# Weighing the values of a head pair in one run of matmuls instead of two

## The chip, the cores and the metric

The kernel runs on one core of one Trainium2 chip. The metric is the time of one execution on the device, in microseconds (us), as the median of several runs. The profile is of one execution taken by the hardware profiler. TensorE, the matmul engine, is called PE in the profile's rows, its weight loads PEld; VectorE is DVE, ScalarE is ACT, GpSimd is POOL, and SP issues DMAs.

## The reference

One inference step of a small diffusion backbone with two layers, over 128 prompt tokens and 512 latent tokens. Each layer normalises its input, projects it, and runs grouped-query attention beside a pooling mixer; an output projection and a gated MLP with a short convolution follow. The attention, which is what the change touches, is this:

```python
def one_block(qi):
    s = jnp.einsum('bqkgd,bskd->bkgqs', qi.astype(jnp.float32), kf) * scale
    p = jax.nn.softmax(s, axis=-1)
    return jnp.einsum('bkgqs,bskd->bqkgd', p, vf).astype(q.dtype)
```

There are 8 query heads of dimension 64 on 2 key heads. A latent block of 128 queries attends to 640 keys: 128 cached ones and 512 latent ones. The prompt's one block attends to its own 128 keys only.

## The kernel before

All tokens lie along the free axis, in five tiles of 128 (tile 0 is the prompt, 1 to 4 the latent tokens). Per layer the program runs the input projection, the attention, the output projection and the MLP, one after the other on TensorE.

The attention is cut into **units**, one for each pair of a query tile b and a head h; `UNITS` lists 40 of them for a layer (`NU`). For each latent tile b there are eight latent units and two prompt units (b equal to 0). A latent unit has five key tiles, a prompt unit one. The prompt units stand as units 0, 1, 14, 15, 24, 25, 34 and 35. Below, a **pair** is two units that follow each other, an even one and the odd one behind it (heads h and h+1 of one tile), named by its even unit.

A unit goes through these operations:

1. `scores(i)` on TensorE (L1781): four matmuls for a latent unit, two for a prompt unit, into the buffer `lin[i % 2]`. It waits until the exponential of unit i-2 is done, which frees the buffer.
2. VectorE takes the row maximum (L1274) and negates and scales it (L1280).
3. ScalarE takes the exponential into `prob[i % 3]` (L853), with the row sum read out behind it (ACTIVATION_READ_ACCUMULATOR).
4. VectorE inverts the sum (L1286) and scales the probabilities (L1288).
5. `transpose_prob(i)` on TensorE (L1794): five transposes (one for a prompt unit) into `pair[2]`. There is one such buffer, so the transposes of unit i wait until ScalarE has emptied it of unit i-1.
6. ScalarE copies it to `prob_place[i % 4]` in SBUF (L866; the rows call it prob_t or tree). This is called the **evacuation** below.
7. `weigh_pair` on TensorE (L1823): for each key tile one matmul for each of the pair's two units, 128 by 64 weights (the values) against 128 columns of transposed probabilities. The two units fill the lower and upper half of the partitions of `pair[3]`. When the last key tile is done, each unit counts up the semaphore `s_o`. These matmuls are fp32, and each leaves two records in the trace, here called passes: 12 for three key tiles, 8 for two, 20 for five. A prompt pair has two matmuls and four passes.

Each engine works its own list in order. On TensorE the list is written by hand, as one loop over **steps** i. Step i weighs, then issues the scores of unit i+2, then transposes unit i-1:

```python
for i in range(NU + 4):
    if i >= 4:
        weigh_pair(i - 4 - i % 2, i % 2)
    if i + 2 < NU:
        scores(i + 2)
    if i in (2, 3):
        keep_busy(2, spare)
    if 1 <= i <= NU:
        transpose_prob(i - 1)
```

So an even step weighs key tiles 0 to 2 of a pair, and the odd step behind it key tiles 3 and 4 of the same pair. For a prompt pair there is only key tile 0, so the odd step weighs nothing. ScalarE's list has, in its turn i, the exponential of unit i and then the evacuation of unit i-2; VectorE's has the maximum of unit i and then the scaling of unit i-1. `keep_busy` issues matmuls whose results nobody reads.

Of the kernel before, what the change touches and what calls it, by code (L numbers as in the profile page):

```python
# [61 lines left out]
def build(nc, x_prompt, x_sample, cache_k, cache_v, c, c_ctx, w_mod, b_mod, norm1_g, w_in,  # L62
# [62 lines left out]
    NU = len(UNITS)  # L125
# [3 lines left out]
    for b in range(1, NT):  # L129
        end = b * (NH + 2) - 1  # L130
        GROUPS += [(1 if b == 1 else end - NH // 2, 0, [b - 1]), (end, b, list(range(NH // 2)))]
    NO = len(GROUPS)
    GROUP_END = {end: i for i, (end, _, _) in enumerate(GROUPS)}

    with ExitStack() as ctx:
# [181 lines left out]
        def o_place(G):  # L317

            _, b, pairs = GROUPS[G]
            at = ((G // 2 + (1 if b == 0 else 0)) % 2) * 512  # L320
            src = pair[3][:, at:at + len(pairs) * P].rearrange("p (t c) -> p t c", t=len(pairs))
            return src, (slice(None), slice(pairs[0], pairs[-1] + 1), slice(b * P, (b + 1) * P))
# [1075 lines left out]
        def _(pe):  # L1398
# [184 lines left out]
            def keep_busy(n, dst=pair[2][:, 0:P]):  # L1583


                for _ in range(n):
                    pe.matmul(dst, ident, ident, start=True, stop=True)  # L1587
# [118 lines left out]
            for L in range(DEPTH):  # L1706
# [60 lines left out]
                def scores(i):  # L1767

                    b, h = UNITS[i]
                    un = L * NU + i  # L1770
                    if i < 2:
                        pe.wait_ge(s_plo, L * NPOOL + NPOOL - 1 + i)
                        pe.wait_ge(s_ks, 4 * (L + 1))
                    else:
                        pe.wait_ge(s_exp, un - 1)
                    pe.wait_ge(s_qs, 2 * L * NQ + h + 1)

                    runs = ((0, 0, 2 * P),) if b == 0 else tuple((TP + a, a, e - a) for a, e in HALVES)
                    for kc, oc, n in runs:
                        for r, kk in enumerate((k_hi, k_lo)):  # L1780
                            ins = pe.matmul(lin[i % 2][:, oc:oc + n], q_st[:, h, b * P:(b + 1) * P],  # L1781
                                            kk[:, h // GRP, kc:kc + n], start=r == 0, stop=r == 1)
                    ins.then_inc(s_s, 1)

                def transpose_prob(i):
                    un = L * NU + i
                    pe.wait_ge(s_prob, un + 1)
                    if i > 0:
                        pe.wait_ge(s_pte, un)
                    else:  # L1790
                        pe.wait_ge(s_val, L + 1)
                        pe.wait_ge(s_kout, L + 1)
                    for kt in range(1 if UNITS[i][0] == 0 else NT):
                        ins = pe.transpose(pair[2][:, kt * P:(kt + 1) * P], prob[i % 3][:, kt * P:(kt + 1) * P], ident)  # L1794
                    ins.then_inc(s_pt, 1)

                def weigh_pair(i, part):

                    b, h = UNITS[i]
                    pos = i // (NH + 2)
                    un = L * NU + i
                    g = h // GRP
                    pe.wait_ge(s_pte, un + 2)
                    if b == 0:

                        if pos > 0:
                            pe.wait_ge(s_olo, L * NO + 2 * pos)
                        c = (pos + 1) % 2 * 512  # L1810
                    else:

                        if h == 0 and pos > 0:
                            pe.wait_ge(s_olo, L * NO + 2 * pos - 1)
                        if h == 0 and pos == 0:
                            pe.wait_ge(s_qsd, 2 * (L + 1))
                        c = (pos % 2) * 512 + h // 2 * P
                    nkt = 1 if b == 0 else NT
                    for kt in range(min(nkt, 3)) if part == 0 else range(3, nkt):
                        vv = val[:, 0, g * HD:(g + 1) * HD] if b == 0 else \  # L1820
                            past[:, 1, g * HD:(g + 1) * HD] if kt == 0 else val[:, kt, g * HD:(g + 1) * HD]
                        for side in range(2):
                            ins = pe.matmul(pair[3][side * HALF:(side + 1) * HALF, c:c + P], vv,  # L1823
                                            prob_place[(i + side) % 4][:, kt * P:(kt + 1) * P],
                                            start=kt == 0, stop=kt == nkt - 1)
                            if kt == nkt - 1:
                                ins.then_inc(s_o, 1)
# [5 lines left out]
                keep_busy(2, spare)  # L1833
                scores(1)
                keep_busy(4, spare)
                for i in range(NU + 4):
                    if i >= 4:
                        weigh_pair(i - 4 - i % 2, i % 2)
                    if i + 2 < NU:
                        scores(i + 2)  # L1840
                    if i in (2, 3):
# [3 lines that stand above are left out]
# [87 lines left out]
```

## Time and profile before

| What | us |
|---|---|
| Median of 3 runs (1461.76 to 1462.82) | 1461.98 |
| The profiled execution, its own time | 1460.13 |
| Its span in the profile | 1458.3 |
| TensorE busy in the span | 1426.2 |
| VectorE busy | 909.5 |
| ScalarE busy | 528.8 |
| GpSimd busy | 390.1 |

The profiled execution's own time is 1.8 us above its span, and the median is 1.9 us above that time. The attention of the first layer lies between about 137 and 217 us of the span, that of the second between about 836 and 916 us. In a timeline row, the first number is the start in us from the span's start, the second the duration, then engine, line, operation, and what it writes and reads; in brackets stands how long the engine sat idle before and who released it, where that is known ("issue" means that the profile shows no one). Rows that follow each other on one line are merged into one with a count (x8).

### The profile page before, as it was taken

Reading aid. Unit: us, or ns where it says so; the run is one execution under the profiler, and the core shown is the slowest. Engines: PE = TensorE matmul, PEld = TensorE weight load, DVE = VectorE, ACT = ScalarE, POOL = GpSimd, SP = SyncE. Lnnn points to the kernel's source line nnn. Section 1 sums busy time; section 2 is a strip of 40 time slices with the busy share of each in tenths; the row PEclk is TensorE's granted clock in tenths of the full one; section 3 lists DMA queues with packets and bytes.
Section 4 is the critical chain, followed back from the end, with each engine's and each line's share of the span. In section 5 each row is a group of like instructions: output and inputs, shape, how many; then the busy total and the mean of one; then the engine's idle time right before and its main releaser. Section 6 shows DMA issues by size and latency. Waiting matters only on the chain.

```text
span 1458.3 us, 25364 instructions
## 1 busy us (share of the span) xinstructions
PE 1426.2 (98%) x10067; PEld 1371.9 (94%) x10067; DVE 909.5 (62%) x1438; ACT 528.8 (36%) x791; POOL 390.1 (27%) x265
## 2 busy tenths in 40 slices
PE   7999999999999999999999999999999999999997
PEld 4888779999999999999999977999999999999997
DVE  3637878897876469785775788259844323444333
ACT  3325872442331122332242578234332112332322
POOL 0145001144431024444214600113423101323321
PEclk9999999999999999999999999999999999999999
DMA  9642004244445324334423200133322222222321
GB/s 342 219 173 77 1 2 145 87 131 140 142 138 154 105 89 158 121 118 153 129 57 86 62 1 1 45 102 116 115 72 83 81 68 73 72 72 72 100 60 73
DMA packets 190719, 147.06 MB, mean 101 GB/s; under 512 B 4256, under 2 KB 178984, under 8 KB 188584
## 3 DMA queue, kind: packets, MB, share of 16 engines
q1 hardware_dynamic: 189152, 144.27, 31.4%
q10 hardware_dynamic: 1480, 1.57, 0.3%
q8 instruction: 62, 1.02, 0.3%
q14 instruction: 25, 0.20, 0.0%
HBM read 142.94 MB, written 2.88 MB: 100 GB/s over the span
## 4 chain that ended last, share of the span: by engine, by line
PE 88%; DVE 7%; ACT 2%; issue 1%; DMA 1%; ACTq 0%; DVEq 0%
PE pair L1404 68%; PE pair L1420 7%; PE pair L1781 3%; PE pair L1823 3%; PE pair L1794 2%; DVE mod_acc L1010 1%; PE pair L1587 1%; DVE in_lo L1076 1%; DVE norm_t L1066 1%; DMA rows<-in_final_norm_g_dram 1%; DVE conv L1326 1%; DVE w_lo L987 1%; PE pair L1702 1%; PE pair L1641 1%; DVE small L1274 1%
## 5 line engine op out<-in xcount | busy, mean ns | idle before, releaser
L1404 PE MATMUL pair<-in_hi,w_hi 128*128 128x384 f32 x1728 | 395.5, 310 | 0.2
L1404 PE MATMUL pair<-in_lo,w_hi 128*128 128x384 f32 x1728 | 393.5, 309 | 0.0
L1404 PE MATMUL pair<-in_hi,w_lo 128*128 128x384 f32 x1728 | 393.4, 309 | 0.0
L1326 DVE SCALAR_TENSOR_TENSOR conv<-pair,vec,conv 128x127 f32<-128x127 f32 x352 | 168.8, 541 | 193.2 <-ACT conv L894 192.9
L1404 PEld LDWEIGHTS pair<-in_hi,w_hi 128*128 128x128 f32 x1728 | 263.6, 188 | 5.3 <-issue 2.9
L1404 PEld LDWEIGHTS pair<-in_lo,w_hi 128*128 128x128 f32 x1728 | 263.7, 188 | 0.0
L1404 PEld LDWEIGHTS pair<-in_hi,w_lo 128*128 128x128 f32 x1728 | 263.7, 188 | 0.0
L602 POOL TENSOR_TENSOR silu_a<-silu_a,conv 128x640 f32<-128x640 f32 x44 | 113.0, 2568 | 534.2 <-DVE conv L1326 534.2
L987 DVE TENSOR_TENSOR w_lo<-w_raw,w_hi 128x1024 fp32r<-128x1024 f32 (+1 forms) x148 | 197.3, 1333 | 64.9 <-ACT w_hi L624 64.6
L894 ACT ACTIVATE conv<-pair,vec 128x640 f32<-128x640 f32 x88 | 77.8, 886 | 407.6 <-PE pair L1404 405.4
L624 ACT ACTIVATE w_hi<-w_raw 128x1024 fp32r<-128x1024 f32 (+1 forms) x82 | 96.9, 1182 | 316.4 <-PE pair L1404 286.1
L1010 DVE SCALAR_TENSOR_TENSOR mod_acc<-mod_raw,cond,mod_acc 128x1024 f32<-128x1024 f32 x112 | 180.1, 1652 | 0.0
L1143 DVE SCALAR_TENSOR_TENSOR x<-pair,mod,x 128x128 f32<-128x128 f32 x80 | 40.3, 545 | 169.5 <-PE pair L1404 169.5
L1404 PE MATMUL pair<-act_hi,w_hi 128*128 128x384 f32 x616 | 140.5, 309 | 0.0
L1404 PE MATMUL pair<-act_hi,w_lo 128*128 128x384 f32 x616 | 140.3, 309 | 0.0
L1404 PE MATMUL pair<-act_lo,w_hi 128*128 128x384 f32 x616 | 140.3, 309 | 0.0
L526 POOL TENSOR_TENSOR ssum<-ssum,sq 128x640 f32<-128x640 f32 x24 | 49.0, 2041 | 309.4 <-ACT sq L648 309.4
L1404 PEld LDWEIGHTS pair<-act_lo,w_hi 128*128 128x128 f32 x616 | 94.0, 188 | 0.0
L1404 PEld LDWEIGHTS pair<-act_hi,w_lo 128*128 128x128 f32 x616 | 94.0, 188 | 0.0
L1404 PEld LDWEIGHTS pair<-act_hi,w_hi 128*128 128x128 f32 x616 | 94.0, 188 | 0.0
L606 POOL TENSOR_TENSOR act_lo<-silu_a,act_hi 128x640 f32 x44 | 84.4, 1919 | 7.5 <-POOL act_hi L604 7.5
L639 ACT ACTIVATE w_hi<-w_raw 128x1024 fp32r<-128x1024 f32 x64 | 67.2, 1050 | 0.0
(198 smaller groups left out, 1805.4 us busy)
## 6 DMA issues: line engine op xcount, KB each, us to landing
w_raw<-in_w_up_dram SPq DMA_DIRECT2D x88, 512.0 KB, 3.7
mod_raw<-in_w_mod_dram SPq DMA_DIRECT2D x64, 512.0 KB, 4.2
w_raw<-in_w_down_dram SPq DMA_DIRECT2D x32, 704.0 KB, 4.6
w_raw<-in_w_in_dram SPq DMA_DIRECT2D x20, 512.0 KB, 3.9
w_first<-in_w_mod_dram SPq DMA_DIRECT2D x8, 1024.0 KB, 14.5
w_raw<-in_w_out_dram SPq DMA_DIRECT2D x16, 512.0 KB, 4.2
mod_raw<-in_w_mod_dram SPq DMA_DIRECT2D x4, 1024.0 KB, 6.6
mod_acc<-in_w_mod_dram SPq DMA_DIRECT2D x4, 1024.0 KB, 6.3
```

The costliest lines, as they stand in the source:

```text
L526: pool.tensor_tensor(ssum[:, :], ssum[:, :], sq_slot(m), ALU.add).then_inc(s_ss, 1)
L602: pool.tensor_tensor(silu_a[:, :], silu_a[:, :], conv[:, 1, :], ALU.mult).then_inc(s_act, 1)
L606: pool.tensor_tensor(act_lo[:, j, :], silu_a[:, :], act_hi[:, j, :].bitcast(F32), ALU.subtract).then_inc(s_alo, 1)
L624: act_e.activation(w_hi[:, s, 0:nk, :], w_raw[:, s, 0:nk, :], ACT.Copy).then_inc(s_whi, 1)
L639: act_e.activation(w_hi[:, s, 0:nk, :], w_raw[:, s, 0:nk, :], ACT.Copy).then_inc(s_whi, 1)
L894: act_e.activation(conv[:, s, :], up_result(g, j, s), ACT.Identity, bias=v(L, V_CONVB, s * NF + g * FG + j), scale=v(L, V_TAP[1], s * NF + ...
L987: dve.tensor_tensor(w_lo[:, s, 0:nk, :], w_raw[:, s, 0:nk, :], w_hi[:, s, 0:nk, :].bitcast(F32), ALU.subtract).then_inc(s_wlo, 1)
L1010: dve.scalar_tensor_tensor(out=mod_acc[:, ci, :], in0=mod_raw[:, s, :], scalar=cond[:, ci, ds(k, 1)], in1=mod_acc[:, ci, :], op0=ALU.mult, ...
L1326: ins = dve.scalar_tensor_tensor(out=conv[:, s, d0:d1], in0=up_result(g, j, s)[:, d0 + sh:d1 + sh], scalar=v(L, V_TAP[t], s * NF + g * FG ...
L1404: ins = pe.matmul(dst[:, a:e], w[:, s, k, :], rhs[:, kk, a:e], start=first and r == 0, stop=last and r == 2)
L1420: ins = pe.matmul(dst[:, a:e], w, rhs[:, a:e], start=start, stop=stop)
L1781: ins = pe.matmul(lin[i % 2][:, oc:oc + n], q_st[:, h, b * P:(b + 1) * P], kk[:, h // GRP, kc:kc + n], start=r == 0, stop=r == 1)
```

## The change

`weigh_pair` loses its second argument. It is called in even steps alone and then runs through all five key tiles of both units; odd steps have only scores and transposes. The loop ends one step earlier, since the last pair is finished in its even step. No operation, buffer or semaphore is added or taken away, and the waits at the head of `weigh_pair` are the same, but are issued once a pair.

```diff
-                def weigh_pair(i, part):
+                def weigh_pair(i):
...
-                    for kt in range(min(nkt, 3)) if part == 0 else range(3, nkt):
+                    for kt in range(nkt):
...
-                for i in range(NU + 4):
-                    if i >= 4:
-                        weigh_pair(i - 4 - i % 2, i % 2)
+                for i in range(NU + 3):
+                    if i >= 4 and i % 2 == 0:
+                        weigh_pair(i - 4)
```

The lists of VectorE, ScalarE and SP are the same as before. On TensorE it looks as follows. First the rows on TensorE in the middle of the first query tile of layer 0, before (prob_t are evacuated probabilities, past and val the cached and new values, sq a probability buffer, cst the identity; 64x128 rows are weighing, each matmul of which gives two records in the trace):

```order
L1794 MATMUL pair<-cst,sq 128x128 x5
L1823 MATMUL pair<-prob_t,past 64x128 x2
L1823 MATMUL pair<-prob_t,val 64x128 x4
L1781 MATMUL pair<-k_hi,q_st 128x384
L1781 MATMUL pair<-k_lo,q_st 128x384
L1781 MATMUL pair<-k_hi,q_st 128x256
L1781 MATMUL pair<-k_lo,q_st 128x256
L1794 MATMUL pair<-cst,sq 128x128 x5
L1823 MATMUL pair<-prob_t,val 64x128 x4
L1781 MATMUL pair<-k_hi,q_st 128x384
L1781 MATMUL pair<-k_lo,q_st 128x384
```

and the same place in the changed kernel:

```order
L1794 MATMUL pair<-cst,sq 128x128 x5
L1822 MATMUL pair<-prob_t,past 64x128 x2
L1822 MATMUL pair<-prob_t,val 64x128 x8
L1781 MATMUL pair<-k_hi,q_st 128x384
L1781 MATMUL pair<-k_lo,q_st 128x384
L1781 MATMUL pair<-k_hi,q_st 128x256
L1781 MATMUL pair<-k_lo,q_st 128x256
L1794 MATMUL pair<-cst,sq 128x128 x5
L1781 MATMUL pair<-k_hi,q_st 128x384
L1781 MATMUL pair<-k_lo,q_st 128x384
```

The four matmuls of key tiles 3 and 4 moved from the odd step to the even one, so that between two runs of transposes there are now only four scores matmuls.

The second place is TensorE in layer 0 where the scores of the prompt units 14 and 15 (two matmuls each) fall into the two steps:

```order
 L1794 MATMUL pair<-cst,sq 128x128 x5
-L1823 MATMUL pair<-prob_t,past 64x128 x2
-L1823 MATMUL pair<-prob_t,val 64x128 x4
+L1822 MATMUL pair<-prob_t,past 64x128 x2
+L1822 MATMUL pair<-prob_t,val 64x128 x8
 L1781 MATMUL pair<-k_hi,q_st 128x256
 L1781 MATMUL pair<-k_lo,q_st 128x256
 L1794 MATMUL pair<-cst,v_feat 128x128 x5
-L1823 MATMUL pair<-prob_t,val 64x128 x4
 L1781 MATMUL pair<-k_hi,q_st 128x256
 L1781 MATMUL pair<-k_lo,q_st 128x256
 L1794 MATMUL pair<-cst,sq 128x128 x5
```

Here only two scores matmuls are left between the transposes.

## Rows read from the trace of the kernel before

**Rows 1.** The page, the chain that ended last: shares of the span by line.

```profile
PE pair L1404 68%; PE pair L1420 7%; PE pair L1781 3%; PE pair L1823 3%; PE pair L1794 2%; DVE mod_acc L1010 1%; PE pair L1587 1%; DVE in_lo L1076 1%; DVE norm_t L1066 1%; DMA rows<-in_final_norm_g_dram 1%; DVE conv L1326 1%; DVE w_lo L987 1%; PE pair L1702 1%; PE pair L1641 1%; DVE small L1274 1%
```

**Rows 2.** Windows (length; busy time of each engine; granted clock), layer 0's attention.

```profile
152.00:216.00 64.00, 61.73 (x568) 49.91 (x568) 50.57 (x140) 51.18 (x109) 0.00 (x0) 1.00 0.01 2
```

**Rows 3.** Timeline, TensorE's weight loads, one even and one odd step of layer 0.

```profile
155.41 0.20 PEld L1823 LDWEIGHTS pair<-prob_t,past 128*64 128x64 f32 x4 [0.17 <-issue]
...
156.21 0.19 PEld L1781 LDWEIGHTS pair<-k_hi,q_st 128*128 128x128 f32 x1 [0.17 <-issue]
...
156.81 0.57 PEld L1794 LDWEIGHTS pair<-cst,sq 128*128 128x128 f32 x5
...
157.54 0.42 PEld L1823 LDWEIGHTS pair<-prob_t,val 128*64 128x64 f32 x8 [0.17 <-issue]
...
158.13 0.19 PEld L1781 LDWEIGHTS pair<-k_hi,q_st 128*128 128x128 f32 x1 [0.17 <-issue]
...
159.46 0.20 PEld L1823 LDWEIGHTS pair<-tree,past 128*64 128x64 f32 x4 [0.17 <-issue]
```

**Rows 4.** Timeline, VectorE and ScalarE at the same place.

```profile
153.44 0.82 DVE L1274 TENSOR_REDUCE small<-pair 128x1 f32<-128x640 f32 x1
...
154.48 0.89 ACT L853 ACTIVATE v_feat<-pair,small,rq 128x640 f32<-128x640 f32 x1
...
155.02 0.82 DVE L1274 TENSOR_REDUCE small<-pair 128x1 f32<-128x640 f32 x1
...
155.27 0.19 ACT L853 ACTIVATION_READ_ACCUMULATOR v_feat<-pair,small,rq 128x1 f32 x1
...
157.10 0.82 DVE L1274 TENSOR_REDUCE small<-pair 128x1 f32<-128x640 f32 x1 [0.41 <-PE pair L1781]
```

**Rows 5.** Timeline, layer 1, an odd step behind a prompt pair, where nothing is weighed.

```profile
873.93 0.58 PEld L1794 LDWEIGHTS pair<-cst,v_feat 128*128 128x128 f32 x5
...
874.78 0.71 ACT L866 ACTIVATE prob_t<-pair 128x640 f32<-128x640 f32 x1
...
874.89 0.19 PEld L1781 LDWEIGHTS pair<-k_hi,q_st 128*128 128x128 f32 x1 [0.39 <-issue]
...
875.60 0.53 PEld L1794 LDWEIGHTS pair<-cst,sq 128*128 128x128 f32 x5
```

**Rows 6.** Timeline, layer 0, four cycles around the prompt pair 14.

```profile
163.52 0.20 PEld L1823 LDWEIGHTS pair<-prob_t,past 128*64 128x64 f32 x4 [0.17 <-issue]
...
164.32 0.19 PEld L1781 LDWEIGHTS pair<-k_hi,q_st 128*128 128x128 f32 x1 [0.17 <-issue]
...
164.57 0.58 PEld L1794 LDWEIGHTS pair<-cst,v_feat 128*128 128x128 f32 x5
...
166.94 0.20 PEld L1823 LDWEIGHTS pair<-tree,past 128*64 128x64 f32 x4 [0.17 <-issue]
...
170.24 0.14 PEld L1794 LDWEIGHTS pair<-cst,v_feat 128*128 128x128 f32 x1
...
170.54 0.20 PEld L1823 LDWEIGHTS pair<-prob_t,past 128*64 128x64 f32 x4 [0.16 <-issue]
...
170.65 0.28 ACT L866 ACTIVATE tree<-pair 128x128 f32<-128x128 f32 x1
...
174.17 0.20 PEld L1823 LDWEIGHTS pair<-tree,val 128*64 128x64 f32 x4 [0.17 <-issue]
...
177.51 0.20 PEld L1823 LDWEIGHTS pair<-prob_t,past 128*64 128x64 f32 x4 [0.17 <-issue]
```

**Rows 7.** Timeline, end of layer 0's attention: weighing of pairs 36 and 38.

```profile
213.51 0.20 PEld L1823 LDWEIGHTS pair<-prob_t,past 128*64 128x64 f32 x4 [0.17 <-issue]
...
216.00 0.20 PEld L1823 LDWEIGHTS pair<-tree,past 128*64 128x64 f32 x4 [0.45 <-ACT tree L866]
```

**Rows 8.** Windows, the start of layer 1's attention.

```profile
842.00:844.00 2.00, 1.12 (x9) 0.88 (x8) 1.90 (x6) 1.54 (x4) 0.00 (x0) 0.97 0.00 0
844.00:846.00 2.00, 2.00 (x11) 2.00 (x10) 1.90 (x5) 1.29 (x5) 0.00 (x0) 0.50 0.00 0
```

## The prediction

> **What bounds the kernel now.** I read the page's chain of waits first, to see whose time the end depends on. Most of it is the large projections (L1404), which the change does not touch. The attention's three lines on TensorE, L1781, L1823 and L1794, are each in the chain with 2 or 3% of the span [rows 1]; what happens to them moves the end. The windows come second: of 64 us of attention TensorE is busy for 61.7, VectorE for 50.6 and ScalarE for 51.2 [rows 2]. So TensorE sets the pace, but the other two are busy four fifths of the time, and a unit goes through all three. The question is thus not only how much work TensorE has, but whether the rhythm of its list suits theirs. That has to be read from the timeline, step by step.
>
> **One cycle (an even and an odd step) as it is** [rows 3], by starts of weight loads. Even step: weighing with 12 passes to the scores, 155.41 to 156.21, 0.80 us; scores 0.60; transposes 0.73 up to the next weighing, of which 0.57 is loading. Odd step: weighing with 8 passes, 157.54 to 158.13, 0.59; then again 0.60 and 0.73. Together 4.05 us, and nobody waits for a semaphore for long: 155.41 to 159.46. From 12 passes in 0.80 and 8 in 0.59 a pass takes 0.0525 us, and what remains at the end of a run is 0.17. The same 0.17 stands as idle time ahead of each weighing and ahead of each scores that follow one [rows 3], but not between scores and transposes. A weighing thus costs its passes and two gaps of 0.17.
>
> **What the change removes.** The odd step's weighing goes, with two gaps: 0.34 us a pair. The 8 passes (0.42 us) only move to the even step. That holds for 15 latent pairs a layer; pair 38 is weighed in one piece now already, since nothing stands between its two parts. If nothing else mattered, 30 pairs by 0.34 would give 10.2 us.
>
> The Trainium skill says in "TensorEngine Tiling (Array Packing)", section Key Properties, that a change of tiling mode (weighing has 64 columns, scores and transposes 128) drains the engine. The 0.17 us agree with that, and by that rule alone the change is a pure gain.
>
> **What it adds: a wait in every odd step.** The transposes of each unit go through one buffer, so between the transposes of unit i-1 and those of unit i lies an evacuation by ScalarE. The kernel before shows this step without weighing already, behind its prompt pairs. There the loads of one unit's transposes end at 873.93 + 0.58 = 874.51, the evacuation runs from 874.78 to 875.49, and the next transposes load at 875.60: 1.09 us after 874.51, of which the scores between them take only 0.60 [rows 5]. The copy itself is 0.71, the hand-over to it 0.27, and back 0.11. There are four such steps between full-size transposes, behind pairs 14 and 24 of each layer; the rows show one, and the other three read the same 1.09. Before, an ordinary odd step puts 0.76 (passes and both gaps) and 0.60 between its transposes, 1.36 in all, so the evacuation is hidden; an even one even more. After, the odd step has 0.60 there and needs 1.09. Of the scores' 0.60 nothing more is won: in-order TensorE stands still for the other 0.49 us. That is the step on which I forecast: the 8 passes were the cover of the evacuation, and they move to a step that had cover already.
>
> **The sum, by kinds of cycle** (weighing start to weighing start).
>
> A: all four operations full size. After: 20 passes and a gap 1.22, scores 0.60, transposes 0.57, evacuation 1.09, transposes 0.57, gap 0.17: 4.22 against 4.05. +0.17, for pairs 4, 6, 16, 26: +0.7.
>
> B: the scores are those of prompt units, 164.57 - 164.32 = 0.25 [rows 6]. After: 1.22 + 0.25 + 0.57 + 1.09 + 0.57 + 0.17 = 3.87; before 163.52 to 166.94, 3.42. +0.45, for 3 pairs (8, 18, 28): +1.35. The wait is longest here, since the shorter scores cover less.
>
> C: the odd step transposes a prompt unit, a single load of 0.14 [rows 6]. After: 1.22 + 0.60 + 0.57 + 1.09 + 0.14 + 0.17 = 3.79; before 3.60 (166.94 to 170.54). +0.19, for 3 pairs: +0.55.
>
> D and E, pairs 12 and 14 and their likes, together 6.97 before (170.54 to 177.51). In D the even step transposes a prompt unit, whose evacuation takes 0.28 instead of 0.70 [rows 6], so the merge saves time there. But then steps follow each other so fast that the softmax chain ends last. From the start of scores to the maximum 0.89 (156.21 to 157.10), from there to the exponential 1.04 (153.44 to 154.48), to the end of its sum 0.98 (to 155.46), back to TensorE 0.11: 3.02 us until the scores two units later may start; two full maxima start 1.58 apart at the closest (153.44 to 155.02) [rows 3, 4]. With the scores of unit 18 at 1.22 after the weighing, those of unit 20 start 3.02 later and those of 21 4.60 later; TensorE's own list would have reached them at 2.5 and about 4.2. Counted from the scores of unit 18, unit 17's transposes end at 3.02 + 0.60 + 0.57 = 4.19, unit 18's wait for the evacuation until 4.19 + 1.09 = 5.28 and end at 5.85, and the next cycle's weighing starts at 1.22 + 5.85 + 0.17 = 7.24. +0.27, with bounds 0 (all chain latencies a little shorter) and +0.6; for three such pairs of cycles +0.8.
>
> End: pair 36, where no scores are left: 1.22 + 0.57 for the last transposes, then the evacuation until pair 38 can be weighed, 0.27 + 0.70 + 0.06: 2.82 against 2.49 [rows 7]. +0.3. Pair 2, at the start, is about 0: there TensorE waits for ScalarE now, and the longer weighing fits into part of that wait.
>
> A layer: 0.7 + 1.35 + 0.55 + 0.8 + 0.3 = 3.7; two layers 7.4. Where the small latencies all come out a few hundredths shorter, A and B lose 0.05 each and D with E 0.1: I take 7.0. The output projection starts right behind the last weighing, and VectorE and ScalarE then wait for its first result, so nothing behind it takes up the delay. The profiled execution would go from 1460.13 to 1467.1 us; the median stands 1.85 above it, 1461.98 + 7.0 = 1469.0.
>
> **Rivals.**
>
> *The gaps win.* If the evacuation were not in the way, the full 0.34 a pair would be back: 1461.98 - 10.2 = 1451.8 us. For it stands that the gaps are real [rows 3]; against it that the step without weighing is in the trace, and waits [rows 5]. It would need an evacuation that starts with the first transpose, and no row shows that. Chance 0.06.
>
> *A draw.* TensorE's own gain and the wait cancel, because the wait is shorter in most odd steps than behind the prompt pairs: with 0.17 less a cycle (0.92 for 1.09), A is 0 and the sum 7.0 - 34 x 0.17 = 1.2 us, thus about 1463. Chance 0.10.
>
> *The clock falls too.* TensorE now stands still a tenth of the time, in C to E more. At the start of layer 1's attention it was busy for 1.12 us of 2, and in the next 2 us the granted clock was 0.50, the lower level of 1.2 GHz; in layer 0's attention it is 1.00 throughout [rows 8, 2]. There half of 2 us of work is lost, 1.0 us. If a fall came with each of the four query tiles of both layers, that is 8 us more: 1477 us. Against it: TensorE will still be busy some 85% of the time. Layer 0's start, where TensorE has little work too, kept its clock. The Trainium skill ("TensorE: Matmul & The Clock Gate", section on a second failure mode) tells of kernels whose frequent short idle times between groups of matmuls made the clock swing; no stretch of this trace with idle times as short as 0.5 us does. Chance 0.10.
>
> **The numbers.** The forecast, 1466 to 1473, has 0.74; the gaps 0.06, the draw 0.10, the clock 0.10. The range takes in half of the draw and the cheaper half of the clock case: 1463.5 to 1475. About 0.2%, 2.9 us, is what a measurement of this kernel can tell from no change; above that, slower, lie the forecast and the clock, 0.84; faster is 0.06, the same 0.10.
>
> **What would show it.** In the profile after: a cycle of kind A of 4.2 us; in every odd step idle time of about 0.5 us ahead of L1794's loads, released by ScalarE's L866, where there is none now; weighing runs of 20 records and 1.22 us; the scores behind transposes start without a gap of 0.17. From the weighing of pair 2 to that of pair 38 some 68.5 us instead of 64.95 in layer 0. The forecast is wrong if odd steps show no such wait, or if the transposes load under 1.0 us behind the previous ones.

## The result, and the profile after

The changed kernel takes 1470.03 us (median of 4 runs, 1467.96 to 1470.53) against 1461.87 us for the kernel before: a ratio of 1.0051, with a 95% interval of 1.0038 to 1.0064. Run a second time on another chip it took 1470.15 us against 1461.88, ratio 1.0049 (1.0036 to 1.0063). The profiled execution took 1467.96 us with a span of 1466.2 us.

The chain that ended last, by line, in the page of the changed kernel; it answers to [rows 1]:

```profile
PE pair L1404 67%; PE pair L1420 7%; PE pair L1822 3%; PE pair L1794 2%; PE pair L1781 2%; DVE mod_acc L1010 1%; PE pair L1587 1%; DVE in_lo L1076 1%; DVE norm_t L1066 1%; ACT prob_t L866 1%; DVE conv L1326 1%; ACT tree L866 1%; DVE small L1274 1%; PE pair L1702 1%; PE pair L1634 1%
```

New in it are ScalarE's evacuations (prob_t and tree, L866). The same shows in the windows of the two attentions (columns as in [rows 2]): TensorE is busy for 60.7 of 69 us, where it was 61.7 of 64, at a full granted clock.

```profile
150.00:219.00 69.00, 60.70 (x588) 51.34 (x587) 51.50 (x145) 52.27 (x111) 0.00 (x0) 1.00 0.01 2
854.00:923.00 69.00, 60.70 (x591) 51.34 (x591) 51.15 (x145) 52.23 (x110) 0.00 (x0) 1.00 0.01 2
```

One full-size cycle in layer 0's timeline, which answers to [rows 3]. Weighing is L1822 now:

```profile
159.15 0.20 PEld L1822 LDWEIGHTS pair<-tree,past 128*64 128x64 f32 x4 [0.17 <-issue]
...
160.39 0.19 PEld L1781 LDWEIGHTS pair<-k_hi,q_st 128*128 128x128 f32 x1 [0.17 <-issue]
...
160.99 0.57 PEld L1794 LDWEIGHTS pair<-cst,sq 128*128 128x128 f32 x5
...
161.52 0.19 PEld L1781 LDWEIGHTS pair<-k_hi,q_st 128*128 128x128 f32 x1
...
161.83 0.70 ACT L866 ACTIVATE prob_t<-pair 128x640 f32<-128x640 f32 x1 [1.00 <-PE pair L1794]
...
162.65 0.53 PEld L1794 LDWEIGHTS pair<-cst,sq 128*128 128x128 f32 x5 [0.48 <-issue]
...
163.35 0.20 PEld L1822 LDWEIGHTS pair<-prob_t,past 128*64 128x64 f32 x4 [0.17 <-issue]
```

The weighing takes 1.24 us; the scores at 161.52 follow the transposes without a gap; and the transposes of the odd step load at 162.65, after 0.48 us of idle time, 1.09 us behind the end of those before (160.99 + 0.57 = 161.56). The loads' row says "issue", but the evacuation ends at 161.83 + 0.70 = 162.53 and they start 0.12 later, the hand-over of [rows 5]. The cycle is 4.20 us, where it was 4.05.

From the weighing of pair 2 to that of pair 38 it is 68.23 us in layer 0 and 68.24 in layer 1 (64.95 and 64.65 before): 6.9 us. Layer 0's pair 2 comes 0.34 earlier. From pair 38 of layer 0 to the first scores of layer 1 it is 621.4 us, where it was 619.8: 1.6 us more, outside the attention. From there to layer 1's pair 2 it is 0.3 less. That makes up the 7.9 us between the two spans; the section on the prediction comes back to the 1.6.

### The profile page after: what moved, and what is told of

It is laid out like the page before. It is cut to its first block, busy times and chain, and to the rows that moved or that the text cites. A ratio compares the mean times of both kernels' runs of the same rounds, so it can differ in the third digit from the quotient of the medians.

```text
span 1466.2 us, 25350 instructions
## 1 busy us (share of the span) xinstructions
PE 1420.0 (97%) x10067; PEld 1371.7 (94%) x10067; DVE 906.9 (62%) x1438; ACT 529.2 (36%) x791; POOL 389.0 (27%) x265
## 3 DMA queue, kind: packets, MB, share of 16 engines
q10 hardware_dynamic: 1480, 1.57, 0.3%
## 4 chain that ended last, share of the span: by engine, by line
PE 86%; DVE 7%; ACT 3%; issue 2%; DMA 1%; SPq 0%; DVEq 0%; ACTq 0%
PE pair L1404 67%; PE pair L1420 7%; PE pair L1822 3%; PE pair L1794 2%; PE pair L1781 2%; DVE mod_acc L1010 1%; PE pair L1587 1%; DVE in_lo L1076 1%; DVE norm_t L1066 1%; ACT prob_t L866 1%; DVE conv L1326 1%; ACT tree L866 1%; DVE small L1274 1%; PE pair L1702 1%; PE pair L1634 1%
## 5 line engine op out<-in xcount | busy, mean ns | idle before, releaser
L602 POOL TENSOR_TENSOR silu_a<-silu_a,conv 128x640 f32<-128x640 f32 x44 | 111.7, 2540 | 536.7 <-DVE conv L1326 536.7
L1010 DVE SCALAR_TENSOR_TENSOR mod_acc<-mod_raw,cond,mod_acc 128x1024 f32<-128x1024 f32 x112 | 179.3, 1646 | 0.7 <-DMA mod_raw<-in_w_mod_dram 0.7
L1274 DVE TENSOR_REDUCE small<-pair 128x1 f32<-128x640 f32 (+1 forms) x80 | 57.0, 713 | 20.8 <-PE pair L1781 20.5
```

Source lines behind the costliest of these rows:

```text
L602: pool.tensor_tensor(silu_a[:, :], silu_a[:, :], conv[:, 1, :], ALU.mult).then_inc(s_act, 1)
L1010: dve.scalar_tensor_tensor(out=mod_acc[:, ci, :], in0=mod_raw[:, s, :], scalar=cond[:, ci, ds(k, 1)], in1=mod_acc[:, ci, :], op0=ALU.mult, ...
L1274: dve.tensor_reduce(small[:, i % 3, 3:4], lin[i % 2][:, 0:nkeys], AX_X, ALU.max).then_inc(s_max, 1)
```

## The experiments

The gap theory says that what counts is the number of changes between 64 and 128 columns of weights. The cover theory says that an evacuation, 1.09 us from transposes to transposes, has to fit under what stands between them. In the tables a cycle is the time from one pair's weighing to the next one's in layer 0's timeline, by kinds as in the prediction; A is the cycle behind pair 4 or 6, E the one behind pair 14. Each ratio is to runs of the kernel before beside it (medians 1461.3 to 1461.9 us), so small differences are better read from the ratios and the cycles than from medians of different chips.

| Kernel | median us | ratio (95%) | A | B | C | D | E |
|---|---|---|---|---|---|---|---|
| before | 1461.87 | 1 | 4.05 | 3.42 | 3.60 | 3.63 | 3.34 |
| changed | 1470.03 | 1.0051 (1.0038 to 1.0064) | 4.20 | 3.85 | 3.75 | 3.33 | 3.86 |
| 4 and 1 key tiles | 1462.84 | 1.0013 (1.0003 to 1.0023) | 4.06 | 3.63 | 3.61 | 3.63 | 3.46 |
| changed, shorter copy | 1466.08 | 1.0031 (1.0018 to 1.0044) | 4.09 | 3.75 | 3.65 | 3.32 | 3.80 |
| before, shorter copy | 1460.01 | 0.9989 (0.9979 to 0.9998) | 4.06 | 3.36 | 3.63 | 3.62 | 3.24 |
| changed, four idle matmuls | 1475.83 | 1.0102 (1.0085 to 1.0118) | 4.60 | 3.84 | 3.76 | 3.33 | 4.70 |
| changed, two idle matmuls | 1471.26 | 1.0060 (1.0046 to 1.0074) | 4.20 | 3.84 | 3.76 | 3.33 | 4.25 |
| changed, scores together | 1472.11 | 1.0068 (1.0051 to 1.0084) | 4.12 | 4.03 | 3.22 | 4.14 | 3.75 |
| changed, shorter maximum | 1467.47 | 1.0044 (1.0027 to 1.0060) | 4.20 | 3.85 | 3.76 | 3.34 | 3.73 |

### Four key tiles and one

```diff
-                    for kt in range(min(nkt, 3)) if part == 0 else range(3, nkt):
+                    for kt in range(min(nkt, 4)) if part == 0 else range(4, nkt):
```

> The kernel before, but with four key tiles in the even step and one in the odd. Number of runs and of gaps as before. Theory (the odd step's transposes wait for the evacuation, 1.09 us from transposes to transposes): the odd step still has 4 passes, two gaps and the scores between transposes, 0.21 + 0.34 + 0.60 = 1.15 us, just over 1.09, so a full-size cycle stays at 4.05 to 4.07 us; where the scores are a prompt unit's 0.25 the cover is 0.80 and the cycle grows from 3.42 to about 3.65. In all +1.5 us, 1463.4. Rival (the long even step itself costs, in proportion to what moves into it): half of the measured loss of the full merge, +4 us, with a full-size cycle of 4.12.

The loads on TensorE in this kernel, weighing of both steps and the odd step's transposes:

```profile
160.36 0.20 PEld L1823 LDWEIGHTS pair<-tree,past 128*64 128x64 f32 x4 [0.17 <-issue]
...
161.97 0.57 PEld L1794 LDWEIGHTS pair<-cst,sq 128*128 128x128 f32 x5
162.71 0.20 PEld L1823 LDWEIGHTS pair<-tree,val 128*64 128x64 f32 x4 [0.17 <-issue]
...
163.68 0.58 PEld L1794 LDWEIGHTS pair<-cst,sq 128*128 128x128 f32 x5
164.42 0.20 PEld L1823 LDWEIGHTS pair<-prob_t,past 128*64 128x64 f32 x4 [0.17 <-issue]
```

From the end of transposes at 162.54 to the next at 163.68 there are 1.14 us, just over the 1.09 of the evacuation, and the cycle has not grown: 4.06. Where the scores are short it grew from 3.42 to 3.63, as expected. The time, +1.2 us, agrees with the cover theory's +1.5. The long even step itself costs nothing.

### A shorter evacuation, in both kernels

```diff
+                        nkeys = min(nkeys, 4 * P)
                         act_e.activation(prob_place[j % 4][:, 0:nkeys], pair[2][:, 0:nkeys], ACT.Copy).then_inc(s_pte, 1)
...
-                                            prob_place[(i + side) % 4][:, kt * P:(kt + 1) * P],
+                                            prob_place[(i + side) % 4][:, min(kt, 3) * P:(min(kt, 3) + 1) * P],
```

> The changed kernel, evacuating only four of five key tiles of a latent unit (the fifth tile of probabilities is left out and the fourth is read in its place; TensorE's work is the same). The copy gets about 0.10 us shorter. Theory: every wait in odd steps gets 0.10 shorter: full-size cycle 4.10, the one with prompt scores 3.76, in all -3.2 to -3.6 us against the changed kernel, about 1466.5. Rival (the loss is in the passes or in the order, not in the copy): no change, 1470.

> The same shorter copy in the kernel before (the fifth tile of probabilities left out). Theory: there the copy is hidden in all cycles but those with prompt scores and those behind prompt pairs: full-size cycle 4.05 as before, in all -1 to -1.8 us, about 1460.5. If the copy were as much in the way as in the changed kernel, -3.5 us, 1458.4.

In the changed kernel with the shorter copy (lines are one further on), an odd step:

```profile
158.17 0.60 ACT L867 ACTIVATE tree<-pair 128x512 f32<-128x512 f32 x1 [0.90 <-PE pair L1795]
...
158.88 0.53 PEld L1795 LDWEIGHTS pair<-cst,v_feat 128*128 128x128 f32 x5 [0.36 <-issue]
```

The copy is 0.60 instead of 0.70, and TensorE's idle time ahead of the transposes 0.36 instead of 0.48. Every kind of cycle with a wait fell by 0.10 to 0.11 (E by 0.06, for a reason that the softmax chain below gives). From pair 2 to pair 38 that is 3.0 us in both layers together; the medians, taken on two chips, differ by 4.0 us. TensorE's work is the same. In the kernel before, the full-size cycle does not answer to the copy at all (4.06), only B and E (and the cycles at the two ends) do, and the time falls by 1.7 us: there the copy is covered. In B it was not quite: the trace of before has 1.09 us from transposes to transposes there too (loads end at 165.15, the next begin at 166.24). This is the plainest of the tests: the same 0.10 us on ScalarE is worth 0.11 in a full-size cycle of one kernel and nothing in the other.

### Idle matmuls in front of the waiting transposes

```diff
+                    if i % 2 and 7 <= i < NU and UNITS[i - 1][0] and UNITS[i - 2][0] and UNITS[i - 3][0] and UNITS[i - 3][1] > 0:
+                        at = ((i - 3) // (NH + 2) % 2) * 512 + UNITS[i - 3][1] // 2 * P
+                        keep_busy(4, pair[3][:, at:at + P])
                     if 1 <= i <= NU:
                         transpose_prob(i - 1)
```

> The changed kernel with four idle matmuls (0.43 us together) ahead of the transposes in 16 odd steps whose two neighbouring transposes are both full size and whose next pair is not the first of its query tile. Theory: TensorE stands still there for 0.48 us anyway, so the time does not change by more than 0.5 us (1470) and the cycles stay 4.20. Rival (TensorE's own work is what has become longer, not a wait): 16 x 0.43 = +7 us, 1477.

Measured were 1475.8 us. The theory's number was off by 6 us; the rival's was close, but by a wrong size of the idle matmuls. The loads of one filled odd step:

```profile
159.11 0.98 PEld L1587 LDWEIGHTS pair<-cst 128*128 128x128 f32 x8
160.00 0.58 PEld L1794 LDWEIGHTS pair<-cst,v_feat 128*128 128x128 f32 x5
```

Four idle matmuls are eight passes and take 0.89 us (159.11 to 160.00), not 0.43. They are fp32 with 128 columns of weights; I had sized them by a stretch in which their records are merged with others. At that size the rival would have been 16 x 0.89 = 14 us; the cycles of the two layers grew by 7.8 together. The full-size cycle grew by 0.40, which is 0.89 less 0.49: the wait paid for the rest. Behind pair 34 no scores are left and the transposes wait the whole 1.09; there the four idle matmuls cost nothing, and the cycle is 3.86 as without them:

```profile
218.82 0.97 PEld L1587 LDWEIGHTS pair<-cst 128*128 128x128 f32 x8
219.95 0.53 PEld L1794 LDWEIGHTS pair<-cst,v_feat 128*128 128x128 f32 x5 [0.15 <-issue]
```

To test that reading and not only to fit it, the same with two:

> As the kernel with four idle matmuls ahead of the transposes in 16 odd steps, but with two. The profile of that kernel shows that an idle matmul is two passes of 0.11 us, so the four were 0.89 us and not 0.43, and a full-size cycle grew by 0.40, which is 0.89 less a wait of 0.49. Two are 0.44 us, just under the wait. Theory: nothing changes, full-size cycle 4.20 to 4.22, total within 0.5 us of the changed kernel beside it. Rival (added work costs a fixed share, 0.45 of its length): +0.20 a cycle, +3.2 us.

```profile
159.01 0.53 PEld L1587 LDWEIGHTS pair<-cst 128*128 128x128 f32 x4
159.56 0.53 PEld L1794 LDWEIGHTS pair<-cst,v_feat 128*128 128x128 f32 x5
160.25 0.20 PEld L1822 LDWEIGHTS pair<-tree,past 128*64 128x64 f32 x4 [0.17 <-issue]
```

Now the transposes follow the idle matmuls almost at once, and the full-size cycle is 4.20 as without them: 0.44 us of work were free. Not free were they behind pair 14 (4.25 for 3.86, the same behind pair 24) and behind pair 2 (4.65 for 4.23), 6 of the 16 places; there most of the wait is elsewhere, ahead of the scores, and has been served when TensorE comes to the transposes (0.39 to 0.42 of the 0.44 is paid). The cycles of the two layers add up to +2.4 us; the median is +1.1 us against the changed kernel beside it on that chip (1470.15), where I had expected under 0.5. The total does not decide against the rival's +3.2, but the cycles do: the added work costs next to nothing or nearly all by its place, not a fixed share.

### The softmax chain

In the changed kernel's timeline, layer 0, the two steps behind the weighing of prompt pair 14 (kind E):

```profile
174.28 0.20 PEld L1822 LDWEIGHTS pair<-tree,val 128*64 128x64 f32 x4 [0.17 <-issue]
175.16 0.19 PEld L1781 LDWEIGHTS pair<-k_hi,q_st 128*128 128x128 f32 x1 [0.69 <-ACT sq L853]
...
175.82 0.53 PEld L1794 LDWEIGHTS pair<-cst,v_feat 128*128 128x128 f32 x5
176.75 0.19 PEld L1781 LDWEIGHTS pair<-k_hi,q_st 128*128 128x128 f32 x1 [0.40 <-ACT sq L853]
...
177.45 0.53 PEld L1794 LDWEIGHTS pair<-cst,sq 128*128 128x128 f32 x5
...
178.14 0.20 PEld L1822 LDWEIGHTS pair<-prob_t,past 128*64 128x64 f32 x4 [0.17 <-issue]
```

Both scores wait for an exponential (sq, L853), the first for 0.69 us. The transposes at 177.45 come 1.10 us behind the end of those before (176.35), about what the evacuation asks, and the scores ahead of them end at about 176.75 + 0.60 = 177.35. So the evacuation ends last there by about 0.1 us only, and both limits act in E; that is why a copy shorter by 0.10 gave only 0.06. The two cycles D and E take 7.19 us, where they took 6.97 [rows 6]. To see whether the chain is what waits there, VectorE's maximum is taken over four of five key tiles:

```diff
-                        dve.tensor_reduce(small[:, i % 3, 3:4], lin[i % 2][:, 0:nkeys], AX_X, ALU.max).then_inc(s_max, 1)
+                        dve.tensor_reduce(small[:, i % 3, 3:4], lin[i % 2][:, 0:min(nkeys, 4 * P)], AX_X, ALU.max).then_inc(s_max, 1)
```

> The changed kernel with the row maximum taken over four of five key tiles (the fifth is left out), 0.13 us shorter on VectorE. Theory: full-size cycles stay 4.20, since the evacuation ends last there; the cycles behind pairs 14, 24 and 34, where the softmax chain ends last, fall from 3.86 to about 3.73; in all -1 us, 1469. Rival (VectorE's load sets the pace everywhere): two maxima a cycle, -0.26 each, -8 us.

The weighing of pair 14 and of pair 16 in that kernel:

```profile
174.37 0.20 PEld L1822 LDWEIGHTS pair<-tree,val 128*64 128x64 f32 x4 [0.17 <-issue]
...
178.10 0.20 PEld L1822 LDWEIGHTS pair<-prob_t,past 128*64 128x64 f32 x4 [0.17 <-issue]
```

3.73 for 3.86, and A, B, C and D as before: the maximum counts in E (and in the first two cycles, by 0.2) and nowhere else. The median is 2.6 us lower, on another chip; against the kernels before beside them the difference is 2.0 us, still more than the 1.2 us that the cycles of both layers add up to, and no larger than the scatter told of below.

The second test of the chain gives every evacuation its cover by the order of the list:

```diff
-                for i in range(NU + 3):
-                    if i >= 4 and i % 2 == 0:
+                for i in range(0, NU + 3, 2):
+                    if i >= 4:
                         weigh_pair(i - 4)
...
+                    if 1 <= i <= NU:
+                        transpose_prob(i - 1)
                     if i + 2 < NU:
                         scores(i + 2)
+                    if i + 3 < NU:
+                        scores(i + 3)
...
-                    if 1 <= i <= NU:
-                        transpose_prob(i - 1)
+                    if i + 1 <= NU:
+                        transpose_prob(i)
```

> The changed kernel with the same work in another order: weighing, transposes, both scores, transposes. Each evacuation is now covered (1.39 us of weighing with its gaps, or 1.20 us of two scores), and TensorE's own list is 3.74 us for a full-size cycle. Theory: not the evacuation but the softmax chain now ends last: the second scores may start only 1.58 + 3.02 = 4.6 us after the first scores of the cycle ahead, which makes full-size cycles of 4.1 to 4.3 us and a total of 1470 to 1473. Rival (only the evacuation stood in the way of the gaps' 0.34 us): cycles of 3.75, total about 1453.

```profile
160.73 0.82 DVE L1274 TENSOR_REDUCE small<-pair 128x1 f32<-128x640 f32 x1 [0.86 <-PE pair L1781]
...
161.76 0.20 PEld L1822 LDWEIGHTS pair<-tree,past 128*64 128x64 f32 x4 [0.17 <-issue]
161.78 0.89 ACT L853 ACTIVATE sq<-pair,small,rq 128x640 f32<-128x640 f32 x1 [0.93 <-DVE small L1280]
...
162.66 0.69 ACT L866 ACTIVATE prob_t<-pair 128x640 f32<-128x640 f32 x1
...
163.47 0.53 PEld L1794 LDWEIGHTS pair<-cst,sq 128*128 128x128 f32 x5 [0.64 <-issue]
```

1472.1 us, full-size cycles of 4.12 to 4.20: not a gain, as the chain theory had it. The rows show one link that I had not named. The transposes wait again (0.64), for an evacuation at 162.66 that stands on ScalarE's list behind an exponential, which waited 0.93 for the maximum of scores issued 1.9 us before. Cover alone does not help when the copy is queued behind the chain. So two things can hold this loop, the evacuation and the softmax chain with ScalarE's list behind it. The full-size cycles of the kernel before waited for neither, and at 4.05 they were as short as this order's.

### The price of a gap

To see that the 0.17 us belong to the change of columns, one idle matmul (128 columns) is set once between the weighing of the two units of a pair and once behind both. Both kernels weigh all key tiles of one unit first, then of the other, in all pairs; 24 pairs have the idle matmul. The diff is of the first; the second has it behind the loop over the two units instead.

```diff
-                    for kt in range(nkt):
-                        vv = ...
-                        for side in range(2):
-                            ins = pe.matmul(...)
+                    for side in range(2):
+                        if side == 1 and b and h < NH - 2 and True:
+                            keep_busy(1, pair[3][:, c + P:c + 2 * P])
+                        for kt in range(nkt):
+                            vv = ...
+                            ins = pe.matmul(...)
```

> The changed kernel, weighing first all key tiles of one unit, then of the other, with one idle matmul of 128 columns of weights between the two for 24 of the pairs. To be read against the next kernel. Theory of the gaps: the idle matmul costs its own 0.11 us and two more gaps of 0.17, 0.45 us a pair in the even step: full-size cycle 4.65, total +10.8 us, 1480.8. Rival (a gap belongs to the semaphore waits ahead of a run, not to the change of the number of columns): +0.11 a pair, cycle 4.31, +2.6 us.

> As the kernel before this one, but with the idle matmul behind the whole weighing, beside the scores, which have the same 128 columns of weights. Both theories: +0.11 us a pair in the even step, full-size cycle 4.31, total +2.6 us, 1472.6. The difference to the kernel before this one is the price of two gaps.

Measured: 1514.4 us (ratio 1.0363, 1.0343 to 1.0383) inside, 1497.9 us (1.0246, 1.0229 to 1.0263) beside. The sizes missed by far, the sign between them held. Inside:

```profile
173.41 0.19 PEld L1824 LDWEIGHTS pair<-tree,past 128*64 128x64 f32 x2 [0.17 <-issue]
173.57 0.90 PEld L1824 LDWEIGHTS pair<-tree,val 128*64 128x64 f32 x8
174.64 0.30 PEld L1587 LDWEIGHTS pair<-cst 128*128 128x128 f32 x2 [0.17 <-issue]
175.06 0.19 PEld L1824 LDWEIGHTS pair<-tree,past 128*64 128x64 f32 x2
175.22 0.90 PEld L1824 LDWEIGHTS pair<-tree,val 128*64 128x64 f32 x8
176.30 0.19 PEld L1781 LDWEIGHTS pair<-k_hi,q_st 128*128 128x128 f32 x1 [0.17 <-issue]
```

and beside:

```profile
172.21 0.19 PEld L1824 LDWEIGHTS pair<-tree,past 128*64 128x64 f32 x2 [0.17 <-issue]
172.38 0.68 PEld L1824 LDWEIGHTS pair<-tree,val 128*64 128x64 f32 x6
172.93 0.19 PEld L1824 LDWEIGHTS pair<-tree,past 128*64 128x64 f32 x2
173.03 0.96 PEld L1824 LDWEIGHTS pair<-tree,val 128*64 128x64 f32 x10
174.16 0.30 PEld L1587 LDWEIGHTS pair<-cst 128*128 128x128 f32 x2 [0.17 <-issue]
174.38 0.19 PEld L1781 LDWEIGHTS pair<-k_hi,q_st 128*128 128x128 f32 x1
```

The idle matmul inside has no semaphore to wait for, and the gap of 0.17 stands before it all the same; behind it, before weighing goes on, another 0.2 (from 174.86, its two passes later, to 175.06). Beside, there is one gap ahead of it and none between it and the scores. So the gap belongs to the change of columns.

Why are both kernels 28 us and more slower? One unit's 10 passes alone take 1.06 us here, 0.106 each, where alternating passes of the two units take 0.0525. Beside, the 20 passes with one gap behind take 1.95 us against 1.24. The plain reading is that the order of the change, key tile by key tile and side by side, lets the two halves of the columns work together. That is not tested apart from a rival: in the other order, matmuls that follow each other also add into the same columns of `pair[3]`. I had not known that this order was worth 0.71 us a pair. Of the difference of 16.5 us between the two kernels, 0.69 us for each of 24 pairs, 0.37 are the two gaps, and the rest is that beside, the second unit's passes can still start beside the first one's last (1.78 us for 20 passes instead of 2.12). The test gave the cause of the gaps, not a clean price; the price is best read as 0.17 from the rows.

### The changed kernel once more

> The changed kernel once more, on the chip of the kernel beside it: 4.20 us for a full-size cycle, total 1468 to 1470.5, ratio to the kernel before 1.005. The runs of the changed kernel so far lie between 1468.0 and 1470.5, those of before within 1.2 us; if the spread sits behind layer 0's attention, where DMAs land just in time, the span between the two attentions differs by 1 to 2 us from one profile to the next and the attentions by less than 0.3.

Median and ratio came as expected. The cycles are the same to 0.04 us but for the last two of layer 1, 4.13 and 4.10 instead of 3.86 and 2.80: together 1.57 us, more than the 0.3 that I had allowed. The windows there:

```profile
918.00:920.00 2.00, 0.86 (x6) 0.68 (x7) 1.50 (x6) 1.88 (x5) 0.00 (x0) 1.00 0.00 0
920.00:922.00 2.00, 2.00 (x17) 1.67 (x18) 0.23 (x1) 0.70 (x1) 0.00 (x0) 0.55 0.00 0
922.00:924.00 2.00, 2.00 (x17) 1.55 (x13) 0.00 (x0) 0.00 (x0) 0.00 (x0) 0.60 0.00 0
```

At the end of the attention, where no scores are left, TensorE was busy for 0.86 of 2 us; then the granted clock was 0.55 and 0.60 over 4 us, the lower of the two levels (1.2 GHz) for most of it. In the first profile of the same kernel it stayed at 1.00 there. The second profile has another fall at the start of layer 1's attention (0.63 and 0.52 from 848 to 852 us), where the kernel before has its own [rows 8].

## Why the prediction was right

The forecast was 1469.0, slower by 7.0; measured were 1470.0, slower by 8.2, and 8.3 in the second comparison.

- **The wait in the odd step** is there as forecast: 1.09 us from transposes to transposes, an idle time of 0.48 (0.49 forecast), no gap between transposes and scores. The shorter copy and the idle matmuls show that it is the evacuation that is waited for.
- **The sum by kinds:** A 4.20 (forecast 4.22), B 3.85 (3.87), C 3.75 (3.79), D with E 7.19 (7.24), the end 2.80 (2.82). Pair 2 fell from 4.36 to 4.23 in layer 0 and rose from 4.09 to 4.24 in layer 1, where I had said about 0 for both. From pair 2 to 38 it is +3.3 us in layer 0 and +3.6 in layer 1, 6.9 in all; 7.4 was summed and 7.0 taken. That 7.0 is a choice and not a sum: taken off every cycle, the allowances that I named make 1.3 us.
- **Nothing behind takes up the delay:** true. But something behind added to it in the profile, and I had not looked for it. From pair 38 of layer 0 to the first scores of layer 1 the twelve profiles here have 619.8 us (four of them, the kernel before among them) or 621.1 to 621.4 (eight, both of the changed kernel among them). (The 0.3 by which the changed kernel's two stand above the other six is mostly a wait of TensorE for ScalarE, 0.3 at L1556.) What parts the eight from the four is one wait of TensorE, the engine that sets the pace, some 93 us behind pair 38, in the MLP. The changed kernel, first profile:

```profile
305.30 3.79 DVE L1010 SCALAR_TENSOR_TENSOR mod_acc<-mod_raw,cond,mod_acc 128x1024 f32<-128x1024 f32 x2
305.46 2.54 POOL L602 TENSOR_TENSOR silu_a<-silu_a,conv 128x640 f32<-128x640 f32 x1 [21.78 <-DVE conv L1326]
...
310.84 1.65 DVE L987 TENSOR_TENSOR w_lo<-w_raw,w_hi 128x1024 fp32r<-128x1024 f32 x1
...
312.54 0.56 PE L1404 MATMUL pair<-in_hi,w_hi 128*128 128x384 f32 x2 [1.42 <-DVE w_lo L987]
```

  and the kernel before at the same place:

```profile
302.09 2.47 DVE L1010 SCALAR_TENSOR_TENSOR mod_acc<-mod_raw,cond,mod_acc 128x1024 f32<-128x1024 f32 x2
302.26 3.74 POOL L602 TENSOR_TENSOR silu_a<-silu_a,conv 128x640 f32<-128x640 f32 x1 [21.76 <-DVE conv L1326]
...
306.31 1.65 DVE L987 TENSOR_TENSOR w_lo<-w_raw,w_hi 128x1024 fp32r<-128x1024 f32 x1
```

  VectorE's two operations L1010 and GpSimd's L602 run at the same time, and one side or the other takes 1.2 to 1.3 us longer, never both. Where it is VectorE, the w_lo behind it is late and TensorE waits for it. In the 24 places (twelve profiles, two layers) the wait of 1.42 to 1.45 us is there in the 11 with the long L1010 and in none of the other 13. It is not bound to the change: the kernel before with the shorter copy has it in layer 0, the changed one with four idle matmuls has it nowhere. The profile of the kernel before has none, the changed kernel's first one (layer 0) and its second two. What tips it is not shown. This wait, worth about 1.3 us each time, and falls of the clock as above are the two sources of scatter that the profiles show; which of them makes the 1.2 between my 7.0 and the 8.2 of the medians stays open, since the runs without a profile do not tell.
- **The rivals.** *The gaps win:* they were saved in fact, but the odd step's wait took 0.49 us where 0.34 were saved and 0.42 of passes moved to the even step, which leaves +0.15 a cycle. Given cover by another order, the loop ran into the softmax chain and the copy queued behind it instead. *A draw:* excluded by the interval; the waits are the same in all odd steps of a kind. *The clock:* not in the middle of the attention, which ran at 1.00 in both profiles of the changed kernel, but at its thin ends. A single fall cost 1.57 us in one profile, more than the 1.0 that I had put down. The Trainium skill (page "TensorE: Matmul & The Clock Gate", section "A second HAM failure mode") tells of a kernel whose frequent short idle times between groups of matmuls made the clock swing. Idle times of 0.48 us in every full-size cycle did not do that here; the fall came after a stretch with idle times of 1.09 and 1.34 us, and the first profile has the same idle times there without a fall.
- **The gaps.** The rule of the Trainium skill that a change of tiling mode drains TensorE ("TensorEngine Tiling (Array Packing)", Key Properties) agrees with the traces, the test with the idle matmul included, with 0.17 to 0.20 us a change. It was right about the gaps and said nothing on who waits for whom.

None of the kernels that compute everything beat the kernel before. Its split into three and two key tiles has 0.76 us of weighing in the odd step, and with the scores' 0.60 that is 1.36 us over an evacuation of 1.09. For a full-size cycle the least that works is about 0.49 of weighing: the split with 0.55 still had a cycle of 4.06.

## What to carry to other kernels

Before two runs of one engine are merged to save what it costs to switch, look at what each of them covers: here the shorter run stood in front of a hand-over through a single buffer, and the merged one stands where nobody needed cover. The trace of before often has the changed step somewhere already (a short unit, the end of a loop); its time from one operation to the next is the best price there is. And a saving on the busiest engine is only worth what is left until the next limit: here the order that was to cover every evacuation had 0.3 us less for TensorE to do in a full-size cycle than the kernel before, and its cycle of 4.12 to 4.20 us was no shorter than the 4.05 of before.

## What the runs showed of the hardware

- Matmuls with 64 columns of weights that alternate between the two halves of the columns take 0.0525 us a pass, those of one half in a row 0.106. That the halves work at the same time when neighbouring instructions alternate is the plain reading, not tested apart.
- A change between 64 and 128 columns costs 0.17 us of idle time on TensorE (0.20 in one place), with or without a semaphore wait; between 128 and 128 columns there is none.
- An fp32 idle matmul of 128 by 128 is two passes of 0.11 us.
- ScalarE's copy out of PSUM takes 0.28 us for 128 columns, 0.60 for 512 and 0.70 for 640; a round trip TensorE, copy, TensorE adds 0.27 + 0.11 (end of the last weight load to the copy, end of the copy to the next load).
- VectorE's L1010 (two operations) took 2.47 us and GpSimd's L602, over the same time, 3.74, or else 3.79 and 2.54. Which of the two came out changed from one profile of a kernel to the next.
